# The experts' down weights of one decoder step, loaded as neighbouring rows per partition

## The chip, the cores and the metric

The kernel runs on one core of a Trainium2 chip. The metric is the device time of one execution in microseconds; before the change it is 1595.35 us, the median of three runs (1594.11 to 1596.82).

## What is computed

The reference is one step of a two-layer decoder over 256 prompt tokens and 8 sample tokens of width 1024, in float32. Layer 0 is gated linear attention and a dense SwiGLU, layer 1 is stick-breaking attention and a top-2-of-8 mixture of SwiGLU experts. Only the experts matter here:

```python
def swiglu(h, w_gate_up, w_down):
    a, b = jnp.split(h @ w_gate_up, 2, axis=-1)
    return (jax.nn.silu(a) * b) @ w_down

# moe_swiglu
for e in range(N_EXPERTS):                     # 8
    y = y + gates[..., e:e + 1] * swiglu(h, w_gate_up[e], w_down[e])
# w_gate_up[e]: (1024, 7168)   w_down[e]: (3584, 1024)   float32
```

One expert's weights are 44.04 MB: 29.36 MB gate and up, 14.68 MB down. Eight of them make 352 MB of the 538 MB that the kernel moves.

## The kernel before, in words

**Stages.** The first 640 us or so are layer 0, the shared keys and values, the attention of layer 1, and the router. Then a branch (L1236) asks if the busiest expert has at most 96 tokens (`CAP`). It has with these inputs, so the first side runs; the other side (L1384 on, with its own reading of the gate and up tiles at L1409) doesn't run here. The experts then run one after the other, in order, up to the last 30 us, which gather the rows back and write the output.

**The ring of tiles.** An expert is cut into 24 tiles (`PER_E`): 16 of gate and up weights (`UP_TILES`) and 8 of down weights. They pass through six SBUF buffers of 16 KB per partition (`e_ring`, `E_RING` = 6), in the order in which TensorE reads them. SyncE issues the loads (L557 to L573): the load of tile j waits until TensorE has read tile j - 6 out (`tile_used`), and `expert_landed` (L468) makes TensorE wait until a tile is there. Three of the six buffers carry the name `ring` in the profile, three `e_ring`.

**Shapes of the tiles.** `load` (L540) makes the access patterns. A gate or up tile holds two blocks of 128 rows of `w_gate_up` and 2048 columns (first half, 512 x 4) or 1536 columns (second half, 384 x 4): a partition gets two runs of 8 KB or of 6 KB. A down tile holds 4, 4, 4, 4, 3, 3, 3, 3 blocks (`DOWN_CHUNKS`) of 128 whole rows of `w_down`: partition p gets rows p, p + 128, p + 256 and so on, runs of 4 KB that lie 512 KB apart in memory.

**Gate and up on TensorE.** `up_rounds` (L1251) multiplies 32 tokens at a time (`ROUNDS` = 3 rounds of `STRIP` = 32) with four strips of the tile's columns, so that four matmuls fill the four 32-column groups of the array side by side. Strip s takes blocks of 32 columns, every fourth one, and lands on PSUM partitions 32 s to 32 s + 31. The gate goes to PSUM banks 0 to 2, the up to banks 3 to 5.

**ScalarE and VectorE between.** ScalarE takes the silu of the gate (L1785), VectorE multiplies with the up part (L2407) and then transposes in blocks of 32 x 32 (L2412), so that the features stand on partitions, in `at`: 28 chunks of 128 features x 96 tokens. This happens twice per expert, for half 0 (16 chunks) and half 1 (12 chunks).

**Down on TensorE.** `rounds` (L1261) takes chunk c of `at` as the weights and the matching 128 rows of the down tile as the moving operand, 12 matmuls of 256 columns per chunk. TensorE waits for `at_kept` (L1361) before down tile 0, for half 0, and before down tile 4, for half 1. The order of loads, matmuls and transposes is written out by hand; there is no planner.

**After an expert.** ScalarE copies the sums to `y_e` (L1792), VectorE multiplies the gates in (L2373), GpSimd writes rows to memory and gathers the next expert's tokens (L686). In the last expert VectorE also adds rows that came back (`early`, L2389), which `turn_early_s` (L1302) on TensorE waits for after down tile 3.

Of the kernel before, what the change touches and what calls it, by code (L numbers as in the profile page):

```python
# [13 lines left out]
P = 128  # L14
# [4 lines left out]
T = TP + NB  # L19
# [3 lines left out]
STRIP = 32  # L23
# [19 lines left out]
ROUNDS = 3  # L43
# [60 lines left out]
UP_TILES = 4 * HALF_TILES  # L104
# [34 lines left out]
def build(nc, A, O, cap=CAP):  # L139
# [3 lines left out]
    with ctx:  # L143
# [43 lines left out]
        pb = [psum[:, i * 512:(i + 1) * 512] for i in range(8)]  # L187
# [27 lines left out]
        crow, at = piece(0, [NC9, D])  # L215
        csilu, at = piece(at, [NC9, D])
        at = 0
        la, at = piece(at, [P, GH, T])
# [5 lines left out]
        cum, at = piece(at, [P, 32, HALF])  # L224
        qd, at = piece(at, [P, 32, HALF])
        kd, at = piece(at, [P, 32, HALF])
        qo, at = piece(at, [P, 16, HALF])
        ko, at = piece(at, [P, 16, HALF])
        qe, at = piece(at, [P, GH, TP])
        dec, at = piece(at, [P, 16])  # L230
# [3 lines left out]
        rT, at = piece(at, [GR, T])  # L234
        ktok, at = piece(at, [P, 2, GH * DK])
        st, at = piece(at, [P, 8, C])
        state = []
        for i in range(2):
            v, at = piece(at, [P, GH, DV])
            state.append(v)  # L240
        k_rows, at = piece(at, [P, NB, DK])
        restart, _ = piece(at, [P, TP])
        rows_kv, at = piece(at, [P, 3 * P])
        ss_o, at = piece(at, [P, 2 * GH + 1])
# [21 lines left out]
        kvtok, at = piece(0, [P, TT, 2 * D], work3)  # L266
        q_row, at = piece(at, [P, D], work3)
# [7 lines left out]
        own, at = piece(at, [P, 8], work3)  # L275
# [81 lines left out]
        def sel(b):  # L357

            return ident[0:NB, b:b + 1].to_broadcast([NB, P])
# [112 lines left out]
        def expert_cols(j, k, lo, n):  # L472

            width = 4 * HALVES[j // (2 * HALF_TILES)][1] if j < UP_TILES else D
            return e_ring[j % E_RING][:, k * width + lo:k * width + lo + n]
# [17 lines left out]
        def _(eng):  # L493
# [46 lines left out]
            def load(j, it):  # L540

                expert, i = it + j // PER_E, j % PER_E
                if i < UP_TILES:
                    lo, width = HALVES[i // (2 * HALF_TILES)]
                    s, k = i % (2 * HALF_TILES) // HALF_TILES, i % HALF_TILES * 2
                    n = 2
                    c = s * FE + lo
                    src = up[expert, k * P:(k + n) * P, c:c + 4 * width]
                else:
                    n = DOWN_CHUNKS[i - UP_TILES]  # L550
                    lo = sum(DOWN_CHUNKS[:i - UP_TILES]) * P
                    width = OUT
                    src = down[expert, lo:lo + n * P, :]
                return (e_ring[j % E_RING][:, 0:n * 4 * width].rearrange("p (k c) -> p k c", k=n),
                        src.rearrange("(k p) c -> p k c", p=P))

            eng.wait_ge(S["kv_stored"], 16 * 6)  # L557
            eng.wait_ge(S["unit_used"], NU)
# [177 lines left out]
        def _(eng):  # L736
# [499 lines left out]
            with eng.If(busiest <= cap):  # L1236
# [13 lines left out]

                def up_rounds(outs, tokens, j, k, width, first, stop):  # L1251

                    pieces = expert_cols(j, k, 0, 4 * width).rearrange("p (c s i) -> p c s i", s=4, i=STRIP)
                    for r in range(ROUNDS):
                        for s in range(4):
                            last = eng.matmul(outs[r][s * STRIP:(s + 1) * STRIP, :].rearrange("p (c i) -> p c i", i=STRIP),  # L1256
                                              tokens[:, r * STRIP:(r + 1) * STRIP], pieces[:, :, s, :], start=first, stop=stop,
                                              skip_group_check=True)
                    return last
# [124 lines left out]
            with eng.Else():  # L1384
                eng.wait_ge(S["expert_rows"], 16)
                eng.wait_ge(S["down_kept"], 1)
                for t in range(TT):
                    n = TOK[t]
                    last = eng.transpose(pb[4][0:NE, t * P:t * P + n], gate_tok[0:n, t, :], ident[0:n, 0:n])
                last.then_inc(S["gateT_done"], 1)  # L1390
                eng.wait_ge(S["gateT_kept"], 1)
                for e in range(NE):
                    if e >= 2:
                        eng.wait_ge(S["gbc_kept"], e - 1)
                    eng.matmul(pb[6 + e % 2][:, 0:T], sel(e), gateT[:], start=True, stop=True).then_inc(S["gbc_done"], 1)
                with eng.Fori(0, NE) as it:
                    for part in range(4):
                        half, s = part // 2, part % 2
                        tiles = range(part * HALF_TILES, (part + 1) * HALF_TILES)
                        for j in tiles:  # L1400
                            expert_landed(eng, it, j)
                        lo, n_chunks = ((0, 16), (16, 12))[half]
                        for n in range(lo, lo + n_chunks):
                            if n >= 2:
                                eng.wait_ge(S["pair_kept" if s else "pair_silu"], it * FEC + (n - 1))
                            else:
                                eng.wait_ge(S["down_kept"], it * 64 + 1)
                            for k in range(KC):
                                last = eng.matmul(pb[2 * s + n % 2][:, 0:T], expert_cols(tiles[k // 2], k % 2, (n - lo) * P, P),  # L1409
                                                  h[:, k, :], start=k == 0, stop=k == KC - 1)  # L1410
                            last.then_inc(S["pair_done" if s else "gate_half_done"], 1)
                    eng.wait_ge(S["pair_kept"], it * FEC + FEC)
                    for i in range(8):
                        j, c0 = UP_TILES + i, sum(DOWN_CHUNKS[:i])
                        expert_landed(eng, it, j)
                        for dc in range(8):
                            n = 8 * i + dc
                            if n >= 4:
                                eng.wait_ge(S["down_kept"], it * 64 + (n - 2))
                            for k in range(DOWN_CHUNKS[i]):  # L1420
                                last = eng.matmul(pb[n % 4][:, 0:T], expert_cols(j, k, dc * P, P), act_m[:, c0 + k, :],
                                                  start=k == 0, stop=k == DOWN_CHUNKS[i] - 1)
                            last.then_inc(S["down_done"], 1)

                sum_squares(FINAL)
                for i in range(2 * TT):
                    t, a = i // 2, i % 2
                    if i == 0:
                        h_is_ready(FINAL)
                    if i >= 2:  # L1430
                        eng.wait_ge(S["y_kept"], i - 1)
                    for j in range(4):
                        last = eng.transpose(pb[4 + i % 2][0:TOK[t], j * P:(j + 1) * P], h[:, 4 * a + j, t * P:t * P + TOK[t]],
                                             ident[:])
                    last.then_inc(S["y_turned"], 1)
# [405 lines left out]
        def _(eng):  # L1841
# [496 lines left out]
            with eng.If(busiest <= cap):  # L2338
# [60 lines left out]
                def one_expert(it, between=((), ())):  # L2399
                    for half in range(2):  # L2400
                        width = HALVES[half][1]
                        by_round = lambda v: v[:, 0:ROUNDS * width].rearrange("p (r c) -> p r c", r=ROUNDS)
                        eng.wait_ge(S["tile_used"], it * PER_E + (half + 1) * 2 * HALF_TILES)
                        eng.wait_ge(S["e_silu"], it * 2 + (half + 1))
                        if half == 1:
                            eng.wait_ge(S["at_kept"], it * 2 + 1)
                        eng.tensor_tensor(by_round(act_e), by_round(silu_e),  # L2407
                                          psum[:, 3 * 512:6 * 512].rearrange("p (r c) -> p r c", r=ROUNDS)[:, :, 0:width],
                                          ALU.mult).then_inc(S["gate_up_kept"], 1)
                        eng.wait_ge(S["gate_up_kept"], it * 2 + (half + 1))  # L2410
                        lo, n = HALVES[half][0] // P, width // STRIP
                        eng.transpose(at[:, lo:lo + n, :].rearrange("p c (r t) -> p r c t", r=ROUNDS),  # L2412
                                      act_e[:, 0:ROUNDS * width].rearrange("p (r c i) -> p r c i", r=ROUNDS, i=STRIP)
                                      ).then_inc(S["at_kept"], 1)
                        for also in between[half]:
                            also()

# [100 lines left out]
```

## Time and profile before

| what | before |
|---|---|
| median of three runs | 1595.35 us |
| the profiled execution | 1586.56 us |
| its span in the trace | 1584.7 us |
| PE busy | 1505.8 us (95%) |
| DVE, ACT, POOL busy | 437.1 us (28%), 326.2 us (21%), 91.2 us (6%) |
| moved by DMA | 538.29 MB, 340 GB/s over the span |
| granted TensorE clock, mean | 0.979 of full |

The span is the time between the first and last record of the core; the execution's own time is 1.9 us longer. PE is TensorE's matmuls and PEld its weight loads; DVE is VectorE, ACT ScalarE, POOL GpSimd, and SPq the queue that SyncE issues loads on. The DMA share is the mean busy share of the core's 16 DMA engines; it can come out a little above 1 where the packets of one engine overlap. GB/s is what all of them moved together. A packet is one contiguous run of bytes that a DMA engine moves.

### The profile page before, as it was taken

How to read it: one execution, taken by the hardware profiler on the slowest of the kernel's cores; microseconds unless marked ns; L12 is line 12 of the kernel's file. 1: busy time of each engine (PE TensorE's matmuls, PEld its weight loads, DVE VectorE, ACT ScalarE, POOL GpSimd, SP SyncE). 2: the span in 40 equal slices, each digit the busy share in tenths (PEclk: the TensorE clock that was granted, in tenths of full speed). 3: DMA queues.
4: the chain of work that ended last, by engine and by line, in shares of the span. 5: the costliest groups of instructions: out<-in, count | busy, mean ns of one | idle time of the engine just before them, and what ended most of it. 6: DMA issues, size and time to landing. Idle time of an engine off the chain costs nothing.

```text
span 1584.7 us, 35720 instructions
## 1 busy us (share of the span) xinstructions
PE 1505.8 (95%) x16405; PEld 895.2 (56%) x16405; DVE 437.1 (28%) x671; ACT 326.2 (21%) x505; POOL 91.2 (6%) x133
## 2 busy tenths in 40 slices
PE   7999899999998989899999999999999999999996
PEld 3994688899898657434435335345244354353353
DVE  4653663455568625200000000010000000000212
ACT  3653353343453534200000000000000000000001
POOL 2001010000004200000000000000000000001000
PEclk9999899999998999899999999999999999999996
DMA  9668778884566895999999999999999999999980
GB/s 345 221 213 302 262 246 272 311 298 156 186 237 256 344 398 215 407 364 396 408 417 410 410 414 412 408 413 404 417 404 406 408 408 409 403 410 411 401 354 30
DMA packets 139783, 538.29 MB, mean 340 GB/s; under 512 B 6572, under 2 KB 29226, under 8 KB 118131
## 3 DMA queue, kind: packets, MB, share of 16 engines
q1 hardware_dynamic: 130322, 504.42, 81.9%
q0 software_dynamic: 8368, 28.32, 4.9%
q10 hardware_dynamic: 944, 3.26, 0.6%
q8 instruction: 131, 2.15, 0.6%
q14 instruction: 18, 0.14, 0.0%
HBM read 521.38 MB, written 14.59 MB: 338 GB/s over the span
## 4 chain that ended last, share of the span: by engine, by line
PE 64%; issue 16%; DMA 12%; DVE 5%; ACT 1%; POOL 0%; SPq 0%; POOLq 0%; DVEq 0%; ACTq 0%
PE psum L1256 31%; PE psum L1268 16%; DMA e_ring<-in_moe_w_gate_up 5%; PE psum L852 3%; PE psum L853 3%; PE psum L854 3%; DMA ring<-in_ada_w 2%; DMA ring<-in_moe_w_gate_up 2%; PE psum L770 1%; DMA e_ring<-in_moe_w_down 1%; DVE w_lo L1859 1%; DVE ring L2211 1%; PE psum L961 1%; DMA xe_rows<-h_rows,row_from 1%; DMA h<-q_scratch 0%
## 5 line engine op out<-in xcount | busy, mean ns | idle before, releaser
L1256 PE MATMUL psum<-e_ring,xe 128*32 128x512 f32 (+1 forms) x3456 | 337.2, 547 | 7.0 <-DMA e_ring<-in_moe_w_gate_up 6.0
L852 PE MATMUL psum<-hh,w_hi 128*128 128x264 f32 x864 | 253.8, 294 | 16.9 <-DVE w_lo L1859 9.0
L1256 PE MATMUL psum<-ring,xe 128*32 128x384 f32 (+1 forms) x2688 | 252.5, 532 | 3.7 <-DMA ring<-in_moe_w_gate_up 3.7
L853 PE MATMUL psum<-hl,w_hi 128*128 128x264 f32 x864 | 248.4, 287 | 0.0
L854 PE MATMUL psum<-hh,w_lo 128*128 128x264 f32 x864 | 248.2, 287 | 0.0
L1256 PEld LDWEIGHTS psum<-e_ring,xe 128*32 128x32 f32 x3456 | 112.5, 110 | 225.9 <-issue 210.0
L1859 DVE TENSOR_TENSOR w_lo<-ring,w_hi 128x1024 fp32r<-128x1024 f32 (+1 forms) x132 | 161.7, 1236 | 145.2 <-ACT w_hi L1460 145.0
L852 PEld LDWEIGHTS psum<-hh,w_hi 128*128 128x128 f32 x864 | 166.4, 193 | 30.8 <-issue 14.0
L1268 PE MATMUL psum<-ring,at 128*32 128x256 f32 x2448 | 180.4, 379 | 0.3 <-DMA ring<-in_moe_w_down 0.3
L1256 PEld LDWEIGHTS psum<-ring,xe 128*32 128x32 f32 x2688 | 87.6, 110 | 164.3 <-issue 156.7
L1269 PE MATMUL psum<-ring,at 128*32 128x256 f32 x816 | 180.1, 379 | 0.0
L2407 DVE TENSOR_TENSOR act_e<-silu_e,psum 128x1536 f32<-128x1536 f32 (+1 forms) x16 | 24.9, 1554 | 539.4 <-PE psum L1256 539.4
L853 PEld LDWEIGHTS psum<-hl,w_hi 128*128 128x128 f32 x864 | 166.8, 193 | 0.0
L854 PEld LDWEIGHTS psum<-hh,w_lo 128*128 128x128 f32 x864 | 165.7, 192 | 0.0
L1460 ACT CAST w_hi<-ring 128x1024 fp32r<-128x1024 f32 (+1 forms) x132 | 135.8, 1034 | 108.1 <-PE psum L854 70.8
L1268 PEld LDWEIGHTS psum<-ring,at 128*32 128x32 f32 x2448 | 101.6, 110 | 70.4 <-issue 3.7
L1268 PE MATMUL psum<-e_ring,at 128*32 128x256 f32 x1584 | 115.6, 379 | 0.4 <-DMA e_ring<-in_moe_w_down 0.4
L1269 PE MATMUL psum<-e_ring,at 128*32 128x256 f32 x528 | 115.5, 379 | 0.0
L1785 ACT ACTIVATE silu_e<-psum 128x1536 f32<-128x1536 f32 (+1 forms) x16 | 20.7, 1292 | 451.5 <-PE psum L1256 451.5
L1268 PEld LDWEIGHTS psum<-e_ring,at 128*32 128x32 f32 x1584 | 65.4, 110 | 45.6 <-DMA e_ring<-in_moe_w_down 1.1
L1269 PEld LDWEIGHTS psum<-ring,at 128*32 128x32 f32 x816 | 89.1, 110 | 0.0
L1766 ACT COPY xe<-psum 128x384 f32<-128x384 f32 x8 | 3.8, 479 | 309.7 <-PE psum L1247 309.7
(402 smaller groups left out, 1249.3 us busy)
## 6 DMA issues: line engine op xcount, KB each, us to landing
e_ring<-in_moe_w_gate_up SPq DMA_DIRECT2D x40, 2048.0 KB, 24.0
ring<-in_moe_w_gate_up SPq DMA_DIRECT2D x24, 2048.0 KB, 25.3
e_ring<-in_moe_w_gate_up SPq DMA_DIRECT2D x32, 1536.0 KB, 17.4
ring<-in_moe_w_gate_up SPq DMA_DIRECT2D x32, 1536.0 KB, 18.3
ring<-in_ada_w SPq DMA_DIRECT2D x20, 2048.0 KB, 11.1
ring<-in_moe_w_down SPq DMA_DIRECT2D x24, 1536.0 KB, 19.7
ring<-in_moe_w_down SPq DMA_DIRECT2D x16, 2048.0 KB, 17.5
e_ring<-in_moe_w_down SPq DMA_DIRECT2D x16, 2048.0 KB
```

What stands on the lines that cost most here:

```text
L770: last = eng.matmul(part_bank(i)[g * STRIP:(g + 1) * STRIP, :], c_pad[:, k, :], cols8(slot("ada", i))[:, at, :], start=half == 0 and i == ...
L852: eng.matmul(to, wh, ah, start=start, stop=False)
L853: eng.matmul(to, wh, al, start=False, stop=False)
L854: return eng.matmul(to, wl, ah, start=False, stop=stop)
L961: last = eng.matmul(pb[g % 2][:, g // 2 * DV:(g // 2 + 1) * DV], k_rows[rows_g, b, :], rows_kv[rows_g, P:3 * P], start=True, stop=True)
L1256: last = eng.matmul(outs[r][s * STRIP:(s + 1) * STRIP, :].rearrange("p (c i) -> p c i", i=STRIP), tokens[:, r * STRIP:(r + 1) * STRIP], pi ...
L1268: eng.matmul(outs[r][strip, :], tokens[:, strip], w, start=start, stop=stop, skip_group_check=True)
L1269: last = eng.matmul(outs[r][CAP:P, :], tokens[:, r * STRIP:(r + 1) * STRIP], rest, start=start, stop=stop, skip_group_check=True)
L1460: eng.copy(unit(w_hi, kind, m, ks), quarter(slot(kind, i), kind, m % 4, ks)).then_inc(S["hi_ready"], 1)
L1785: eng.activation(silu_e[:, 0:ROUNDS * width].rearrange("p (r c) -> p r c", r=ROUNDS), psum[:, 0:ROUNDS * 512].rearrange("p (r c) -> p r c" ...
L1859: eng.tensor_tensor(unit(w_lo, kind, m, ks), quarter(slot(kind, i), kind, m % 4, ks), unit(w_hi, kind, m, ks), ALU.subtract).then_inc(S["l ...
L2407: eng.tensor_tensor(by_round(act_e), by_round(silu_e), psum[:, 3 * 512:6 * 512].rearrange("p (r c) -> p r c", r=ROUNDS)[:, :, 0:width], AL ...
```

## The change

The down tiles are read with the pattern `(p k) c -> p k c` in place of `(k p) c -> p k c`: partition p now gets rows 4p to 4p + 3 of the tile's 512 rows (or 3p to 3p + 2 of 384). These lie side by side in memory, as one run of 16 KB (or 12 KB), and side by side in the partition.

So the features must stand in `at` in the same order. The strips of `up_rounds` are now four runs of 128 (or 96) neighbouring columns each, one per group c of 512 (or 384) features. The transposition becomes three instructions, one for each round of 32 tokens. Each reads the columns of `act_e` with a stride of 4 (or 3) elements, so that chunk k of group c holds features 4p + k (or 3p + k) of the group. The branch that doesn't run gets the same order through `up_columns`. Down matmuls, PSUM use, waits and counts of semaphores stay as they are.

```diff
@@ load @@
                 return (e_ring[j % E_RING][:, 0:n * 4 * width].rearrange("p (k c) -> p k c", k=n),
-                        src.rearrange("(k p) c -> p k c", p=P))
+                        src.rearrange("(k p) c -> p k c" if i < UP_TILES else "(p k) c -> p k c", p=P))
@@ up_rounds @@
-                    pieces = expert_cols(j, k, 0, 4 * width).rearrange("p (c s i) -> p c s i", s=4, i=STRIP)
+                    pieces = expert_cols(j, k, 0, 4 * width).rearrange("p (c s i) -> p c s i", c=4, s=4)
                     for r in range(ROUNDS):
                         for s in range(4):
-                            last = eng.matmul(outs[r][s * STRIP:(s + 1) * STRIP, :].rearrange("p (c i) -> p c i", i=STRIP),
+                            last = eng.matmul(outs[r][s * STRIP:(s + 1) * STRIP, :].rearrange("p (c i) -> p c i", c=4),
                                               tokens[:, r * STRIP:(r + 1) * STRIP], pieces[:, :, s, :], start=first, stop=stop,
                                               skip_group_check=True)
@@ the branch that does not run @@
+                def up_columns(j, k, chunk, n):
+                    return expert_cols(j, k, chunk // n * n * P, n * P).rearrange("p (c n) -> p n c", n=n)[:, chunk % n, :]
+
...
-                                last = eng.matmul(pb[2 * s + n % 2][:, 0:T], expert_cols(tiles[k // 2], k % 2, (n - lo) * P, P),
+                                last = eng.matmul(pb[2 * s + n % 2][:, 0:T], up_columns(tiles[k // 2], k % 2, n - lo, n_chunks // 4),
                                                   h[:, k, :], start=k == 0, stop=k == KC - 1)
@@ one_expert on VectorE @@
                         lo, n = HALVES[half][0] // P, width // STRIP
-                        eng.transpose(at[:, lo:lo + n, :].rearrange("p c (r t) -> p r c t", r=ROUNDS),
-                                      act_e[:, 0:ROUNDS * width].rearrange("p (r c i) -> p r c i", r=ROUNDS, i=STRIP)
-                                      ).then_inc(S["at_kept"], 1)
+                        for r in range(ROUNDS):
+                            turned = eng.transpose(at[:, lo:lo + n, r * STRIP:(r + 1) * STRIP].rearrange("p (c k) t -> p c k t", c=4),
+                                                   act_e[:, r * width:(r + 1) * width].rearrange("p (c i k) -> p c k i", c=4, i=STRIP))
+                        turned.then_inc(S["at_kept"], 1)
```

## Rows read from the trace of the kernel before

**Rows 1.** The page, part 2: DMA's share and GB/s in 40 slices.

```profile
DMA  9668778884566895999999999999999999999980
GB/s 345 221 213 302 262 246 272 311 298 156 186 237 256 344 398 215 407 364 396 408 417 410 410 414 412 408 413 404 417 404 406 408 408 409 403 410 411 401 354 30
```

**Rows 2.** Timeline of ACT: start, us, instruction; one keeping per expert.

```profile
774.80 0.80 ACT L1792 COPY y_e<-psum 128x768 f32<-128x768 f32 x1 [7.86 <-PE psum L1269]
...
1102.90 0.80 ACT L1792 COPY y_e<-psum 128x768 f32<-128x768 f32 x1 [7.86 <-PE psum L1269]
...
1213.85 0.80 ACT L1792 COPY y_e<-psum 128x768 f32<-128x768 f32 x1 [7.86 <-PE psum L1269]
...
1437.06 0.80 ACT L1792 COPY y_e<-psum 128x768 f32<-128x768 f32 x1 [7.86 <-PE psum L1269]
...
1553.46 0.80 ACT L1792 COPY y_e<-psum 128x768 f32<-128x768 f32 x1 [51.20 <-PE psum L1269]
```

**Rows 3.** Waits, 1102.9 to 1554 us: total us, times, longest.

```profile
PEld psum L1256 <- DMA e_ring<-in_moe_w_gate_up: 14.7, 12, 2.3
...
PEld psum L1268 <- DMA e_ring<-in_moe_w_down: 1.1, 2, 0.9
```

**Rows 4.** DMA issues of expert 2, then of expert 4: KB, us to landing.

```profile
e_ring<-in_moe_w_gate_up SPq DMA_DIRECT2D x5, 2048.0 KB, 18.1
...
e_ring<-in_moe_w_gate_up SPq DMA_DIRECT2D x5, 2048.0 KB, 23.9
```

**Rows 5.** Windows of experts 2 and 4, all engines, DMA share and GB/s.

```profile
core 0: us, PE busy (x) PEld busy (x) DVE busy (x) ACT busy (x) POOL busy (x), PEclk, DMA share, GB/s
786.00:800.00 14.00, 14.00 (x136) 4.29 (x132) 0.00 (x0) 1.45 (x1) 0.00 (x0) 1.00 1.01 421
812.00:834.00 22.00, 22.00 (x264) 8.45 (x260) 3.53 (x2) 1.13 (x1) 0.00 (x0) 1.00 1.01 415
842.00:868.00 26.00, 26.00 (x456) 14.69 (x452) 2.73 (x2) 0.00 (x0) 0.00 (x0) 1.00 1.02 408
1010.00:1022.00 12.00, 12.00 (x120) 3.62 (x116) 0.00 (x0) 1.45 (x1) 0.00 (x0) 1.00 1.01 419
1030.00:1052.00 22.00, 22.00 (x264) 8.45 (x260) 3.53 (x2) 1.13 (x1) 0.00 (x0) 1.00 1.01 415
1066.00:1090.00 24.00, 24.00 (x452) 14.46 (x448) 2.51 (x2) 0.00 (x0) 0.00 (x0) 1.00 1.03 410
```

**Rows 6.** The page, parts 2 and 3: packets and queues.

```profile
DMA packets 139783, 538.29 MB, mean 340 GB/s; under 512 B 6572, under 2 KB 29226, under 8 KB 118131
...
q1 hardware_dynamic: 130322, 504.42, 81.9%
...
q8 instruction: 131, 2.15, 0.6%
```

**Rows 7.** Chain of waits, 1500 to 1560 us: start, us, what.

```profile
1503.69 22.83 DMA e_ring<-in_moe_w_down
...
1553.46 0.81 ACT y_e L1792
```

**Rows 8.** Groups by form, 640 to 1584 us: count, busy us, mean ns.

```profile
L1256 PE MATMUL psum<-e_ring,xe 128*32 128x512 f32 x1920 | 211.9, 597 | 7.0 <-DMA e_ring<-in_moe_w_gate_up 6.0 <-DVE xe L2369 0.9
L1268 PE MATMUL psum<-ring,at 128*32 128x256 f32 x2448 | 180.4, 379 | 0.3 <-DMA ring<-in_moe_w_down 0.3
...
L2412 DVE STREAM_TRANSPOSE at<-act_e 128x1536 f32<-128x1536 f32 x8 | 14.2, 1778 | 0.3
```

**Rows 9.** Chain of waits, expert 2 up to the start of expert 3.

```profile
774.66 72.16 PE psum L1256 x768
...
884.02 72.16 PE psum L1256 x768
```

**Rows 10.** Timeline of DVE, expert 2, then the last expert.

```profile
848.43 1.38 DVE L2412 STREAM_TRANSPOSE at<-act_e 128x1152 f32<-128x1152 f32 x1
...
1518.73 1.27 DVE L2397 SCALAR_TENSOR_TENSOR back<-back,w_early 8x1024 f32<-8x1024 f32 x1
```

## The prediction

> **What bounds the kernel now.** I read the page first, then the timeline of ScalarE, the waits by stretch, the DMA issues with their landing times, and the windows.
>
> The page shows the DMA engines busy from slice 19 of 40 to slice 39 (713 to 1545 us), at 396 to 417 GB/s and 354 in the last of them [rows 1]. So the experts run with the memory stream full. Whether it also sets the pace is seen at the copies of `y_e`, one at the end of each expert. From expert 1 to expert 4 three periods take 1102.90 - 774.80 = 328.1 us, 109.37 each [rows 2]. In these TensorE waits for no DMA. The next takes 110.95, the two after it 223.21 together, the last 116.40. Over four times 109.37 that is 1.58 + 4.47 + 7.03 = **13.1 us**, the time that TensorE stands and waits for tiles in experts 5 to 8. The waits name it [rows 3]: nearly all before gate and up tiles, only 1.1 us before down tiles. The wait's place says only where the delay came to light: in expert 2 a 2 MB tile landed 18.1 us after its issue, in expert 4 after 23.9 [rows 4]. TensorE needs some 5 us for such a tile (48 records at 211.9 / 1920 = 0.110 us, [rows 8]) and a load is issued five tiles ahead, so some 25 us are there. The stream thus falls behind TensorE through all experts, and the 13.1 us are what was left when the lead was used up. The last wait ends at 1503.69 + 22.83 = 1526.5 us [rows 7]; from there TensorE runs the last 27 us to 1553.5 alone, 20 of the 28 down chunks.
>
> So there are two clocks: TensorE's floor of 109.37 us per expert, and the stream, a little slower. A faster stream pays for each microsecond up to 1526.5, and at most 13.1 us in all.
>
> **What the stream pays for a run's length.** The windows take stretches in which one kind of tile is under way and GpSimd writes nothing [rows 5]. In the order of the loads these are half-0 tiles (8 KB runs: 421 and 419 GB/s), half-1 tiles (6 KB: 415, 415) and down tiles (4 KB: 408, 410), each with a DMA share of 1.01 to 1.03. At 420 GB/s over 16 engines an 8 KB packet takes 312.1 ns, at 409 a 4 KB packet 160.2 ns. A line through both has 37.97 ns for 1 KB and **8.3 ns for each packet**; it gives 236.1 ns for 6 KB, and 415 GB/s make 236.9. So the line holds for the third point. Estimates from it: 16 KB in 615.9 ns (425.6 GB/s), 12 KB in 464.0.
>
> **The change part by part.**
> *Down loads.* A tile of four blocks had 4 x 128 / 16 = 32 packets of 4 KB per engine and will have 8 of 16 KB, each saving 3 x 8.3 = 24.9 ns. A tile of three goes from 24 to 8 of 12 KB, each saving 16.6 ns. With four tiles of each, an expert's down part is shorter by 32 x 24.9 + 32 x 16.6 = 1328 ns, 1.33 us. Up to the last wait there are seven whole experts and the three tiles of the eighth that TensorE has waited for by then: (7 x 32 + 24) x 24.9 = 6.2 us and 7 x 32 x 16.6 = 3.7 us, together **9.9 us**. The windows are read to whole GB/s: with 408 and 421 the packet costs 9.8 ns and the sum is 11.7 us, with 410 and 419 it is 6.8 ns and 8.1 us. That the 4 KB packets gain nothing is the lower end of the cost's bounds, a packet free of any cost (8.3 ns more on each remaining one) the upper, and there the 13.1 us cap it.
>
> The skill weighs this term otherwise. The Trainium skill, DMA: Bandwidth & Descriptors, "Why small descriptors are slow", gives some 3 cycles per packet, which at its 850 MHz of the fabric ("Where 436 GB/s comes from") is an estimate of 3.5 ns; the sum would be 4.2 us instead of 9.9. The rows show more than twice that, so I go by them.
>
> *Issues.* SyncE issues as many loads as before, of the same size and behind the same waits. No queue is passed by another, and GpSimd's writes and gathers stay where they are. Longer packets on SyncE's queue can delay a gather's short ones by some 0.3 us each time the engine changes queues (615.9 against 312.1 ns); a gather is needed a whole expert later. No cost.
>
> *Gate and up matmuls.* Same count, same columns. In runs of 32 they take 110.4 ns a record for 512 columns, 0.216 ns per column. The down matmuls read 256 neighbouring columns; L1268 with its quarter at L1269 has 3264 records in 180.4 us, 55.3 ns for 256, 0.216 too [rows 8]. Length of run costs nothing in either direction: zero.
>
> *Transpositions.* One of 1536 elements takes 1778 ns, one of 1152 takes 1379 [rows 8, 10], so 1.04 ns per element and 182 ns for the instruction. Two more instructions add 0.36 us to each half. The stride of 3 or 4 elements isn't in the trace. The bounds are no cost and, reading four times as slowly, 5.3 us more; I take none, as the rows nearest to it are the same instruction. Neither matters: half 0's is done some 27 us before its tile. Half 1's ends at 849.8 in expert 2 [rows 10]. Down starts there at 774.66 + 72.16 = 846.8, and tile 4 is due 16 chunks of up to 1.33 us later ((884.02 - 846.82) / 28, [rows 9]), so at 868: 18 us of cover. What queues behind it on VectorE is the copy of the next tokens, due later still. In the last expert `early(2)` follows, ends at 1520.0 [rows 10] and is needed about 1537, after down tile 3. If the cover were gone, each microsecond over it would stop TensorE once per expert.
>
> **The sum.** 9.9 us off the profiled execution's 1586.56 (span 1584.7 and 1.9 around it) makes 1576.7. The median of the runs, 1595.35, is 8.8 above that execution. I carry the difference over: **1585.5 us**. What is late next is still the stream, by 13.1 - 9.9 = 3.2 us, in the last expert.
>
> **The rivals.**
> *The 8.8 us lie on TensorE.* If the runs without a profile have a slower TensorE over the experts, the stream waits there already and only 13.1 - 8.8 = 4.3 us are left to win: 1591.0. For it: the gap is larger than the spread of the runs (2.7 us). Against: a gap outside the experts, or in the stream, leaves my sum whole.
> *The packets cost nothing at 4 KB.* 409 against 420 GB/s may come from where the runs lie in memory, not from their length. Then nothing moves: 1595.4. Against it is the third point on the line. The same page of the Trainium skill ("Specifications") puts the smallest transfer for line rate at 512 B, which by itself says this case. The trace disagrees by 11 GB/s between 4 and 8 KB. The same result comes if the loads are still cut into 4 KB runs; then q1 keeps its 130322 packets [rows 6].
> *Long runs are slow: slower than before.* Sixteen engines would each read a long piece of one block that lies together, where now each run of a partition lies 512 KB from the next. The only 16 KB packets of this trace, the 131 of q8, take 0.006 x 16 x 1584.7 / 131 = 1.16 us each [rows 6], not 0.62. They load instructions, so I don't take them as a price: at it the 248 packets of 16 KB and 224 of 12 KB (three quarters) would cost 248 x 520 + 224 x 390 ns = 216 us. The point from which this case decides is 641 ns (four times 160.2). A mild form, the 396 GB/s that is the lowest inner slice of the stage [rows 1], is 662 ns, so 21.2 ns over, 248 x 21.2 + 224 x 15.9 = 8.8 us: 1604.2.
> *The stream gains more than TensorE allows.* Packet cost of 11 ns or more: 13.1 us, 1582.3.
>
> **How the numbers follow.** The packets' line is measured at three lengths and the wait it feeds is measured too: 0.60 for the forecast, whose own range is 1583.5 to 1587.5. 0.05 for the full 13.1 us, 0.13 for a slower TensorE, 0.14 for no gain, 0.08 for slower. A change of 0.2% is 3.2 us, about what a measurement of this kernel can tell from none: faster 0.60 + 0.05 + 0.13 = 0.78, same 0.14, slower 0.08. The range takes the cap with 1 us of spread at the low end, 1581.3, and holds the slower TensorE with the same spread at the high end, 1592; that is 0.78 of the cases.
>
> **What would show it.** q1 should have 20480 packets fewer (8 x 8 tiles: 28672 become 8192), and those under 8 KB 28672 fewer. Windows over down tiles should show about 425 GB/s, over gate and up tiles the same as before. Periods between the `y_e` copies should stay at 109.4 us up to expert 6 or 7, with some 3 us of waits for DMA in all, and the 2 MB tiles of expert 4 should land in about 20 us. L1256 should keep 0.216 ns per column. Transpositions should be 48, a third as long, with no wait of TensorE on them. I am wrong if the down windows stay at 409 GB/s, if the waits fall and the periods don't, or if TensorE's floor itself moves.

## The result and the profile after

| | before | after |
|---|---|---|
| median | 1595.39 us (10 runs) | 1583.30 us (10 runs) |
| lowest to highest | 1590.36 to 1596.82 | 1579.38 to 1588.65 |
| the profiled execution | 1586.56 us | 1586.65 us |
| its span | 1584.7 us | 1584.8 us |

The ratio after to before is 0.9937, with a 95% interval of 0.9923 to 0.9951: faster by 0.6%. The medians stand 12.1 us apart, the ratio makes it 10.1 (7.8 to 12.3). The profiled execution of the kernel before is not among its ten runs.

The two profiled executions are equally long, though. That has to be taken apart first. The timeline of ScalarE has the ends of the experts (start, us, instruction), to be read against [rows 2]:

```profile
784.29 0.80 ACT L1795 COPY y_e<-psum 128x768 f32<-128x768 f32 x1 [7.86 <-PE psum L1269]
...
1112.39 0.80 ACT L1795 COPY y_e<-psum 128x768 f32<-128x768 f32 x1 [7.86 <-PE psum L1269]
1221.76 0.80 ACT L1795 COPY y_e<-psum 128x768 f32<-128x768 f32 x1 [7.86 <-PE psum L1269]
...
1440.49 0.80 ACT L1795 COPY y_e<-psum 128x768 f32<-128x768 f32 x1 [7.86 <-PE psum L1269]
1552.02 0.80 ACT L1795 COPY y_e<-psum 128x768 f32<-128x768 f32 x1 [50.03 <-PE psum L1269]
```

From expert 1's end to expert 8's there are now 767.73 us, and there were 778.66: **10.9 us** less. Expert 1 ends 9.5 us later (784.29 against 774.80), and from expert 8's end to the end of the span there are 32.8 us instead of 31.2. Of the 9.5 us, 7.4 lie before the first expert's first load (at 636.15 us instead of 628.76), in code that the change does not touch. The windows of 150 to 190 us (all engines, PEclk, DMA share, GB/s), first of the kernel before:

```profile
150.00:160.00 10.00, 7.35 (x64) 2.86 (x64) 4.97 (x12) 3.19 (x2) 2.26 (x3) 1.00 1.00 358
160.00:170.00 10.00, 8.65 (x68) 4.49 (x65) 6.05 (x14) 1.04 (x1) 1.50 (x2) 0.93 1.05 404
170.00:180.00 10.00, 4.70 (x31) 2.73 (x30) 7.78 (x13) 6.71 (x11) 1.49 (x2) 0.67 0.77 282
180.00:190.00 10.00, 10.00 (x76) 10.00 (x76) 6.44 (x13) 2.94 (x4) 0.00 (x0) 0.89 0.58 211
```

and of the kernel after:

```profile
150.00:160.00 10.00, 8.65 (x52) 2.82 (x48) 3.31 (x8) 3.42 (x3) 1.51 (x2) 0.66 1.00 344
160.00:170.00 10.00, 8.70 (x54) 3.71 (x50) 4.72 (x10) 1.04 (x1) 1.50 (x2) 0.66 0.95 317
170.00:180.00 10.00, 6.18 (x51) 3.10 (x52) 6.86 (x12) 2.16 (x5) 2.25 (x3) 0.95 0.99 341
180.00:190.00 10.00, 5.94 (x29) 5.17 (x28) 5.75 (x10) 4.55 (x7) 0.00 (x0) 0.54 0.19 55
```

The granted clock has two levels here, full (2.4 GHz) and half (1.2 GHz), and PEclk is their mean over the window. The clock records of the trace show half for 10.2 of these 40 us in the execution before and for 23.9 in the one after. SyncE's later loads are then some 7 us later all the way. The other ten profiled executions fit: two more have a short time at half (13.7 us) and reach the first expert's first load at 631.9 and 632.6 us, the other eight have 19.2 to 26.1 us and reach it at 634.7 to 638.9.

The other 2.1 us lie between that load and expert 1's end: 148.1 us, and 146.0 before. The change is at work there already, but loads alone and order alone, the first two experiments below, take 145.8 and 146.6. Between 640 and 770 us the execution after has 17.1 us at half clock, the one before 10.2. In the eleven profiled executions without the longer delay on VectorE of the last experiment, expert 1 ends between 774.80 us (the kernel before, the earliest of all) and 785.56, and the time after expert 8 is 30.4 to 32.8 us, which I haven't taken apart. So the page's own time of one execution can't show this change; the periods between the experts can.

The waits of TensorE for weight tiles in the experts (total us, times, longest), against [rows 3]:

```profile
PEld psum L1256 <- DMA e_ring<-in_moe_w_gate_up: 3.9, 2, 2.2
PE psum L1256 <- DMA e_ring<-in_moe_w_gate_up: 2.0, 2, 1.3
```

The landing of expert 4's 2 MB tiles (DMA issues), against [rows 4]:

```profile
e_ring<-in_moe_w_gate_up SPq DMA_DIRECT2D x5, 2048.0 KB, 15.5
```

The packets on the page, against [rows 6]:

```profile
DMA packets 119302, 538.29 MB, mean 340 GB/s; under 512 B 6571, under 2 KB 29225, under 8 KB 89458
...
q1 hardware_dynamic: 109842, 504.42, 81.1%
```

Every period is 109.37 us but the last, 111.53. So 2.2 us are left of the 13.1 that experts 5 to 8 had over that floor. The tiles land in 15.5 us instead of 23.9, and q1 has 20480 packets fewer. The windows over the down tiles in experts 2 and 4, at the times of before, against [rows 5]:

```profile
842.00:868.00 26.00, 26.00 (x401) 12.81 (x397) 3.30 (x4) 0.11 (x1) 0.00 (x0) 1.00 1.00 424
...
1066.00:1090.00 24.00, 24.00 (x398) 12.64 (x392) 3.30 (x4) 0.00 (x0) 0.00 (x0) 1.00 1.00 424
```

The same stretches, moved on by the 10 us that the experts start later:

```profile
852.00:878.00 26.00, 26.00 (x464) 14.83 (x460) 3.30 (x4) 0.00 (x0) 0.00 (x0) 1.00 1.00 421
...
1072.00:1098.00 26.00, 26.00 (x472) 15.08 (x468) 3.30 (x4) 0.00 (x0) 0.00 (x0) 1.00 1.00 421
```

The groups by form, against [rows 8]:

```profile
L1256 PE MATMUL psum<-e_ring,xe 128*32 128x512 f32 x1920 | 211.9, 598 | 2.9 <-DMA e_ring<-in_moe_w_gate_up 2.0 <-DVE xe L2372 0.9
L1268 PE MATMUL psum<-ring,at 128*32 128x256 f32 x2448 | 180.4, 379 | 0.0
...
L2416 DVE STREAM_TRANSPOSE at<-act_e 128x512 f32<-128x512 f32 x24 | 25.8, 1130 | 0.3
L2416 DVE STREAM_TRANSPOSE at<-act_e 128x384 f32<-128x384 f32 x24 | 15.6, 701 | 0.3
```

By the packets in the trace, the first two windows hold down tiles alone, since the stream has more lead now: 424 GB/s instead of 408 to 410. The two that are moved on have 10 to 12% of their bytes in the next expert's 8 KB runs, and 421. Over gate and up tiles the forecast was the same rate as before. Two windows over 8 KB runs have 423 and 426 GB/s (796 to 808, 1015 to 1027 us), where 421 and 419 stood. Two over 6 KB runs have 405 and 411 (822 to 840, 1030 to 1052), where 415 stood. That dip wasn't forecast and isn't taken apart. The matmuls' busy time is the same to the digit. Only the transpositions have grown, from 14.2 and 11.0 us to 25.8 and 15.6 over the eight experts.

### The profile page after: what moved, and what is told of

It is laid out like the page before. It is cut to its first block, busy times and chain, and to the rows that moved or that the text cites. A ratio compares the mean times of both kernels' runs of the same rounds, so it can differ in the third digit from the quotient of the medians.

```text
span 1584.8 us, 35752 instructions
## 1 busy us (share of the span) xinstructions
PE 1511.8 (95%) x16405; PEld 897.9 (57%) x16405; DVE 453.1 (29%) x703; ACT 326.2 (21%) x505; POOL 91.2 (6%) x133
## 4 chain that ended last, share of the span: by engine, by line
PE 70%; issue 17%; DMA 6%; DVE 4%; ACT 2%; POOL 0%; SPq 0%; ACTq 0%; POOLq 0%; DVEq 0%
PE psum L1256 35%; PE psum L1268 18%; PE psum L852 3%; PE psum L853 3%; PE psum L854 3%; PE psum L770 2%; DMA e_ring<-in_moe_w_gate_up 2%; DMA ring<-in_ada_w 2%; DVE w_lo L1862 1%; PE psum L961 1%; DVE ring L2214 1%; PE psum L817 1%; DMA xe_rows<-h_rows,row_from 1%; PE psum L1269 1%; DMA h<-q_scratch 0%
## 5 line engine op out<-in xcount | busy, mean ns | idle before, releaser
L1256 PE MATMUL psum<-e_ring,xe 128*32 128x512 f32 (+1 forms) x3456 | 337.2, 548 | 2.9 <-DMA e_ring<-in_moe_w_gate_up 2.0
L852 PE MATMUL psum<-hh,w_hi 128*128 128x264 f32 x864 | 253.8, 294 | 17.1 <-DVE w_lo L1862 9.2
L1256 PE MATMUL psum<-ring,xe 128*32 128x384 f32 (+1 forms) x2688 | 251.8, 531 | 0.0
L1256 PEld LDWEIGHTS psum<-e_ring,xe 128*32 128x32 f32 x3456 | 113.0, 111 | 221.2 <-issue 216.1
L852 PEld LDWEIGHTS psum<-hh,w_hi 128*128 128x128 f32 x864 | 166.3, 192 | 31.2 <-issue 15.8
L1256 PEld LDWEIGHTS psum<-ring,xe 128*32 128x32 f32 x2688 | 87.6, 110 | 159.8 <-issue 159.8
L2410 DVE TENSOR_TENSOR act_e<-silu_e,psum 128x1536 f32<-128x1536 f32 (+1 forms) x16 | 24.9, 1554 | 519.0 <-PE psum L1256 519.0
L1463 ACT CAST w_hi<-ring 128x1024 fp32r<-128x1024 f32 (+1 forms) x132 | 135.8, 1034 | 109.1 <-PE psum L854 70.9
L770 PE MATMUL psum<-ring,c_pad 128*32 128x512 f32 x512 | 66.9, 637 | 1.8 <-DMA ring<-in_ada_w 1.8
```

Of the source, the lines that this page charges most:

```text
L770: last = eng.matmul(part_bank(i)[g * STRIP:(g + 1) * STRIP, :], c_pad[:, k, :], cols8(slot("ada", i))[:, at, :], start=half == 0 and i == ...
L852: eng.matmul(to, wh, ah, start=start, stop=False)
L1463: eng.copy(unit(w_hi, kind, m, ks), quarter(slot(kind, i), kind, m % 4, ks)).then_inc(S["hi_ready"], 1)
L2410: eng.tensor_tensor(by_round(act_e), by_round(silu_e), psum[:, 3 * 512:6 * 512].rearrange("p (r c) -> p r c", r=ROUNDS)[:, :, 0:width], AL ...
```

## The experiments

For each kernel the text gives the excess: the time from expert 1's end to expert 8's, less 7 x 109.37 = 765.6 us. It leaves the clock of the early stages out. It is 13.1 us for the kernel before and 2.1 for the changed one. Where nothing waits it is -0.3, as the last period then is 109.1. It comes from one profiled execution of each kernel. Each ratio is to runs of the kernel before that were taken beside it; their medians are 1593.38 us for the first three experiments, 1593.28 for the runs of 2, 4 and 16 KB and 1594.96 for the rest.

**Loads alone.** The kernel before, with this line:

```diff
-                        src.rearrange("(k p) c -> p k c", p=P))
+                        src.rearrange("(k p) c -> p k c" if i < UP_TILES else "(p k) c -> p k c", p=P))
```

> The kernel before with the change to load alone: down tiles in runs of 16 or 12 KB, matmuls and the one transposition as before. The features of at then meet the wrong rows of the down weights. Theory (the stream pays 8.3 ns for each packet, and nothing else in the change matters): as fast as the changed kernel, 0.9937 of before within 0.002; no more than 3 us of waits for DMA on TensorE in the experts; down windows at about 424 GB/s. Rival (part of the gain comes from the gate and up matmuls' longer runs or from the transpositions): less than 7 us faster than before.

Measured: 1583.86 us, ratio 0.9939 (0.9915 to 0.9962), excess 1.8 us. Down windows show 426 and 425 GB/s (842 to 868 and 1066 to 1090 us). The whole gain is there, without the change's matmuls and transpositions.

**Order alone.** The changed kernel with that line taken back.

> The changed kernel with the old load: matmuls and the three strided transpositions per half as changed, down tiles in runs of 4 KB. The features of at then meet the wrong rows of the down weights. Theory: as before, ratio 1.000 within 0.002, with the 13 us of waits for DMA back and down windows at 409 GB/s. Rival (the new order helps TensorE or costs VectorE time on the path): a ratio off 1 by more than 0.002, with periods between the y_e copies other than 109.4 us in experts 1 to 4.

Measured: 1595.89 us, ratio 1.0016 (1.0001 to 1.0032), excess 12.6 us. The periods (timeline of ScalarE) are those of before:

```profile
1113.50 0.80 ACT L1795 COPY y_e<-psum 128x768 f32<-128x768 f32 x1 [7.86 <-PE psum L1269]
1224.48 0.80 ACT L1795 COPY y_e<-psum 128x768 f32<-128x768 f32 x1 [7.86 <-PE psum L1269]
1335.60 0.80 ACT L1795 COPY y_e<-psum 128x768 f32<-128x768 f32 x1 [7.86 <-PE psum L1269]
1446.24 0.80 ACT L1795 COPY y_e<-psum 128x768 f32<-128x768 f32 x1 [7.86 <-PE psum L1269]
1563.63 0.80 ACT L1795 COPY y_e<-psum 128x768 f32<-128x768 f32 x1 [51.15 <-PE psum L1269]
```

Expert 5 takes 110.98 us where it took 110.95. The ratio sits just above 1 (the medians are 2.5 us apart), but nothing in the experts has grown, so I take the order as free there. Where the 2.5 us lie wasn't tried.

**Where the cap is.** The changed kernel with half of each down run loaded:

```diff
-                        src.rearrange("(k p) c -> p k c" if i < UP_TILES else "(p k) c -> p k c", p=P))
+                to = e_ring[j % E_RING][:, 0:n * 4 * width]
...
+                return to[:, 0:n * D // 2], src.rearrange("(p k) c -> p (k c)", p=P)[:, 0:n * D // 2]
```

> The changed kernel, loading only the first half of each partition's down run (8 or 6 KB instead of 16 or 12 KB), so half of the down weights are stale data. Theory (TensorE's floor caps the gain at 13.1 us in the experts, and the change already took about 11 of them): no wait for DMA in the experts at all, all periods 109.4 us, 2 to 3 us faster than the changed kernel, ratio to before about 0.992. Rival (TensorE is slowed by the stream itself, so that less traffic speeds it up): periods below 109 us and a ratio below 0.985.

Measured: 1580.72 us, ratio 0.9921 (0.9897 to 0.9944), excess -0.3 us and no wait for a weight tile. With 59 MB less to load, the periods stay at 109.37: TensorE isn't slowed by the stream, and the experts have 13.1 + 0.3 = 13.4 us to give, of which the change took 10.9.

**Length or place.** In a series of five kernels every down load leaves out one sixty-fourth of its columns, so that runs can't join, and the number of runs is free. Bytes are the same in all. `m` is 1, 2, n or 2n runs per partition and tile:

```diff
+                of = n * D // m
+                return (to.rearrange("p (m c) -> p m c", m=m)[:, :, 0:of - of // 64],
+                        src.rearrange("(p k) c -> p (k c)", p=P).rearrange("p (m c) -> p m c", m=m)[:, :, 0:of - of // 64])
```

The fifth keeps the rows 512 KB apart: `to[:, :, 0:D - D // 64], src[:, :, 0:D - D // 64]` with the old pattern.

> One of a series in which every down load leaves out one sixty-fourth of its columns, so that neighbouring rows can't join: here 4032 bytes of each 4 KB row, four or three neighbouring rows per partition (those columns are stale data). 224 packets per engine and expert in down, as before. The bytes left out alone are worth 14.68 MB / 64 / 409 GB/s = 0.56 us per expert, 4.2 us in all. Theory (packet count sets the cost, place in memory nothing): down windows at 406 to 410 GB/s, as the same series with rows apart, ratio to before about 0.9974. Rival (it is the place in memory that helps, not the length): down windows at 420 GB/s or more and a ratio near 0.992.

> The same bytes (4032 of each 4 KB row), with the rows of a partition 512 KB apart as in the kernel before; matmuls and transpositions as changed, so features meet the wrong rows. Theory: no difference to the neighbouring rows in time (within 2 us) or in the down windows (within 3 GB/s). Rival: 8 us slower than these, and 10 GB/s lower in the down windows.

> The same bytes and the same memory as the neighbouring rows, in runs of 2016 bytes: 448 packets per engine and expert in down. Theory (8.3 ns a packet): 224 x 8.3 = 1.86 us more per expert than runs of 4032 bytes, 13.8 us in all up to the last wait; ratio to before about 1.006; down windows near 390 GB/s. Rival (no cost for a packet of 2 KB or more): as runs of 4032 bytes, ratio 0.997.

> The same bytes in one run per partition, of 16128 or 12096 bytes: 64 packets per engine and expert in down. Theory: the stream is 4.2 + 9.9 = 14.1 us shorter than before, more than TensorE's floor allows, so 0.992 of before, as with half of the down weights not loaded, and no or under 1 us of waits for DMA; down windows at 424 GB/s. Rival (place in memory): no faster than the neighbouring rows in runs of 4032 bytes.

> Again one sixty-fourth of the columns left out, in two runs per partition, of 8064 or 6048 bytes: 128 packets per engine and expert in down. Theory: 96 x 8.3 = 0.80 us less per expert than runs of 4032 bytes, 5.9 us up to the last wait, and 10.1 us less than before: ratio 0.9937; down windows at about 418 GB/s. Rival (no cost for a packet): as runs of 4032 bytes, ratio 0.997.

| run, bytes | packets per engine and expert | median us | ratio (95%) | excess us |
|---|---|---|---|---|
| 16128 / 12096 | 64 | 1581.93 | 0.9917 (0.9885 to 0.9948) | -0.3 |
| 8064 / 6048 | 128 | 1586.19 | 0.9944 (0.9923 to 0.9966) | 3.4 |
| 4032, near | 224 | 1592.87 | 0.9996 (0.9976 to 1.0017) | 12.3 |
| 4032, 512 KB apart | 224 | 1592.04 | 0.9994 (0.9978 to 1.0010) | 12.9 |
| 2016 | 448 | 1605.87 | 1.0078 (1.0048 to 1.0107) | 25.4 |

The windows of 852 to 868 us, in expert 2's down tiles, one kernel each; runs of 16 KB,

```profile
852.00:868.00 16.00, 16.00 (x276) 8.84 (x272) 3.31 (x4) 0.00 (x0) 0.00 (x0) 1.00 1.01 426
```

of 8 KB,

```profile
852.00:868.00 16.00, 16.00 (x280) 8.97 (x276) 3.30 (x4) 0.00 (x0) 0.00 (x0) 1.00 1.01 415
```

of 4 KB from neighbouring rows,

```profile
852.00:868.00 16.00, 16.00 (x288) 9.12 (x284) 3.30 (x4) 0.00 (x0) 0.00 (x0) 1.00 1.03 402
```

of 4 KB with the rows apart,

```profile
852.00:868.00 16.00, 16.00 (x304) 9.65 (x300) 1.91 (x3) 0.00 (x0) 0.00 (x0) 1.00 1.03 403
```

and of 2 KB.

```profile
852.00:868.00 16.00, 16.00 (x290) 9.24 (x286) 3.31 (x4) 0.00 (x0) 0.00 (x0) 1.00 1.05 381
```

Place in memory makes no difference that shows: near and apart differ by 1 GB/s and by 0.6 us of excess. Length does. From 224 to 448 packets the excess grows by 13.1 us where 13.8 were expected from 8.3 ns, so 7.9 ns for a packet; from 224 to 128 it falls by 8.9, where 5.9 were, so 12.5 ns. By the windows a 4 KB row takes 160.5 ns (4032 x 16 / 402) in one packet and 169.3 ns in two, 8.8 ns for the one added. The windows over the longer runs hold about as many bytes of three-block tiles as of four-block ones, by the packets in the trace. So a row comes there in 0.59 packets (8 and 6 KB runs, 415 GB/s, 155.5 ns) or in 0.29 (16 and 12 KB runs, 426 GB/s, 151.4 ns): 5.0 ns for 0.41 packets and 9.1 ns for 0.71, 12 to 13 ns a packet. So this series has a packet at 8 to 9 ns between 2 and 4 KB, and at 12 to 13 ns from 4032 bytes up. The window of the 2 KB runs was expected near 390 GB/s and has 381.

One step failed, for the short runs. The left-out bytes should have been worth 4.2 us by themselves (ratio 0.9974), and the two kernels with runs of 4032 bytes show only 0.2 to 0.8 us less excess than before, and 0.9996 and 0.9994. Their windows, expected at 406 to 410 GB/s, have 402 and 403, so a packet of 4032 bytes takes 160.3 ns (at 402.5), as long as one of 4096 took (160.2). That is part of the 12 to 13 ns: these packets cost more than their bytes. The longer runs did get shorter. The kernel with 8 KB runs has 9.7 us less excess than before, where 10.1 were expected with the left-out bytes counted. And packets of 12096 bytes take 456.8 ns (mean of their records in the trace, 700 to 1500 us), where those of 12288 take 465.0 in the changed kernel. What keeps a run of 4032 bytes at the time of 4096 stays open.

The Trainium skill, DMA: Bandwidth & Descriptors, "How a descriptor splits into AXI transactions", cuts a run into transactions of 256 bytes and a leftover. By it 4032 and 4096 bytes both are 16 transactions, and 12096 and 12288 both are 48. The trace has the first pair equal and the second 8.2 ns apart, so the number of transactions alone doesn't give the time here.

**The cover of the transpositions.** The changed kernel with one more instruction on VectorE ahead of half 1's transpositions (12, then 20 in place of 12):

```diff
+                        if half == 1:
+                            eng.tensor_reduce(tmp8[:, 0, 0:1], act_e[:, 0:ROUNDS * width].unsqueeze(1).to_broadcast([P, 12, ROUNDS * width]),
+                                              AX.XY, ALU.add)
```

> The changed kernel with one added instruction on VectorE in half 1 of each expert, ahead of the transpositions, that sums act_e 12 times over into an element of tmp8 that nothing reads before it is written again: about 12 x 1.2 = 14.4 us. Theory (at is needed 17 to 18 us after VectorE starts the transpositions, and these take 2.1): covered, so as the changed kernel within 2 us, no wait of TensorE for VectorE at down tile 4. Rival (the transpositions are on the path, or VectorE's reads slow the matmuls): some microseconds more per expert, over 20 us in all.

> The same with 20 sums, about 24 us of VectorE. Theory: cover of about 17 us less 2.1 for the transpositions is exceeded by some 9 us in each expert; periods between the y_e copies near 118 us instead of 109.4, and 65 to 75 us more than the changed kernel. Rival (the cover is wider than worked out): less than 30 us more.

The first delay: 1582.00 us, ratio 0.9910 (0.9887 to 0.9933), excess 1.7 us, no wait for VectorE. Its timeline of VectorE in expert 2:

```profile
857.80 1.35 DVE L2410 TENSOR_TENSOR act_e<-silu_e,psum 128x1152 f32<-128x1152 f32 x1 [25.98 <-PE psum L1256]
859.19 14.55 DVE L2416 TENSOR_REDUCE tmp<-act_e 128x1 f32<-128x13824 f32 x1
873.66 1.94 DVE L2419 STREAM_TRANSPOSE at<-act_e 128x384 f32<-128x384 f32 x3
```

The second: 1656.38 us, ratio 1.0389 (1.0361 to 1.0418), 61.4 us over the kernel before and 73 over the changed one, excess 66.9 us. Its timeline of VectorE in expert 2:

```profile
860.54 24.15 DVE L2416 TENSOR_REDUCE tmp<-act_e 128x1 f32<-128x23040 f32 x1
884.61 1.81 DVE L2419 STREAM_TRANSPOSE at<-act_e 128x384 f32<-128x384 f32 x3
```

And that of TensorE, with the wait in brackets:

```profile
886.48 0.65 PE L1268 MATMUL psum<-e_ring,at 128*32 128x256 f32 x3 [6.83 <-DVE at L2419]
```

TensorE stands at tile 4 for 6.83 us, and its matmuls start 7.0 us late (the last one before started at 879.24, the next was due 0.22 us later). That is less than the 9 us that were expected. The rest comes from the clock, in the windows behind the wait:

```profile
885.00:890.00 5.00, 3.52 (x36) 1.69 (x40) 1.42 (x3) 0.00 (x0) 0.00 (x0) 0.51 0.53 220
890.00:895.00 5.00, 5.00 (x84) 2.57 (x79) 0.00 (x0) 0.00 (x0) 0.00 (x0) 0.81 0.13 25
```

The trace has the granted clock at half from 885.1 to 891.9 us, after TensorE has stood since 879.6, and the matmuls follow each other in 0.43 us instead of 0.22. Over the 5.4 us from 886.5 that is 2.7 us more. Together 9.7, the 119.06 - 109.37 of this period. The periods are 117.7 to 119.7 us, 8.3 to 10.3 over the floor. So `at` was due 18.9 us after VectorE was free to transpose (879.46 - 860.54). With the changed transpositions' 1.95 us, 17 us of cover are left, against the 18 that were worked out. The first delay of 14.55 us stays inside and costs nothing; 24.15 us cost some 9.7 per expert, 7 as the wait and 3 as the clock.

## Why the prediction was right

The forecast was 1585.5 us, measured are 1583.3, in the range and on the side with the chance of 0.78. Step by step:

*The bound.* Right. The stream's shortfall shows as the excess of the periods, what came off the stream came off the time, and the cap stands where it was put: 13.1 us forecast, 13.4 measured with half of the down weights left out.

*The packet's price.* Right in kind, close in size. The sum had 9.9 us for 1192 packets per engine; the experts gave 10.9, or 9.2 ns for a packet instead of 8.3. The windows with down tiles alone show 424 GB/s for the 425.6 and 424 of the estimate; that is 154.6 ns for 4 KB, 5.6 less than 160.2 for the 160 of 224 packets that are gone, so 7.9 ns a packet. The price came from three lengths inside one trace, two of them in gate and up tiles. The windows that it was read from weren't of one kind throughout: those of 1010 and 1066 us have about a tenth of their bytes in another run length, which moves them by about 1 GB/s. The series at equal bytes bears out a price of this size, 8 to 9 ns between 2 and 4 KB, and has more, 12 to 13 ns, from the costly 4032-byte runs up. The Trainium skill, DMA: Bandwidth & Descriptors, "Why small descriptors are slow", has 3 cycles for a packet, an estimate of 3.5 ns, which would have made 4.2 us: too little by more than half, as the forecast chose.

*The gap of 8.8 us.* Carrying it over was right, and the rival that put it on TensorE in the experts falls. All periods without a wait are 109.37 in both kernels, and the order alone has these periods and 12.6 us of excess in an execution of 1596.60 us, longer than the median. Most of the profiled execution's lead of 8.8 us lay before the experts, as the ends of expert 1 show. That the granted clock makes this difference is read from the traces, and wasn't tried by itself. That before and after have equal profiled executions was chance: 9.5 us more up to expert 1's end, 10.9 less in the experts, 1.5 more behind them.

*No cost at 4 KB, or only the place.* Falls with the equal times of near and apart rows and with the slower 2 KB runs. The Trainium skill, DMA: Bandwidth & Descriptors, "Specifications", has 512 B as the smallest transfer for line rate. That didn't hold in this stream: 2016-byte runs cost 25.4 - 12.3 = 13.1 us against 4032-byte ones.

*Long runs slow.* Didn't happen; the q8 packets were, as said, no price for these.

*Matmuls and order.* Zero in the experts, as taken: L1256 has 211.9 us in 1920 records before and after, and the order alone changed no period.

*Transpositions.* The wrong term, hidden by its cover. "A third as long" failed: that would be 593 ns for 512 elements, and they take 1130. I took no cost for the stride and had 532 ns for 512 elements beyond the 182 for the instruction. With the stride of 4 it is 1130 - 182 = 948 ns, 1.85 ns per element instead of 1.04; with the stride of 3 701 - 182 = 519 ns, 1.35 per element. The bounds held (up to four times), and the cover made it worth nothing. No run changes the stride by itself: the new instructions are also shorter and take their blocks in another order. So the stride as the cause is argued, not shown. A rule speaks to this that I hadn't weighed: the Trainium skill, SBUF — State Buffer, Door 1: The DMA port swizzle, notes lines of 16 bytes, where each access that crosses into a new line pays. Four floats apart, every access does; three apart, three of four do. The trace has both slower, in that order. The same note has 4 floats as how far one can stride for free; with 3 the trace's time per element is 30% longer already.

*Late next.* The 3.2 us that were to be left are 2.2, in the last expert, as said.

*What the profile should show.* q1's packets came out exactly, the periods hold to expert 7, and TensorE's waits for tiles (3.9 us on PEld) are near the 3 that were said. Expert 4's tiles land in 15.5 us, not about 20: the lead of the stream is larger than the sum made it, and I haven't taken that apart.

## What to carry to other kernels

Where a kernel's memory stream and its engine run neck and neck, compare the periods of a repeated piece of work with and without waits: their excess is what a faster stream can give, and its cap. Read the price of a packet from windows over different run lengths in the same trace; look first at which tiles a window holds. Here the price is 8 to 9 ns on each engine, so going from 4 KB to 16 and 12 KB made the down tiles' stream about 4% faster (424 GB/s for 408 to 410), and it counts only up to the cap. And check a gain of 0.6% in the stage that it is meant for, since a single profiled execution can hide it whole.

## What was not expected of the hardware

A packet of 4032 bytes took as long as one of 4096 (160.3 and 160.2 ns), so trimming these runs saved nothing, while packets of 12288 bytes got 8.2 ns shorter when 192 bytes were trimmed. The transposition of 32 x 32 blocks in VectorE goes from 1.04 to 1.35 and 1.85 ns per element when it reads 3 and 4 floats apart. A wait of TensorE of 7 us cost 2.7 us more through the granted clock, which stood at half for 6.8 us around its end. And in two executions of the same early code the granted clock was at half for 10.2 and for 23.9 us between 150 and 190 us. The later execution ended expert 1 9.5 us later, nearly the size of the effect under study.
